# Two out-projection pieces moved into the recurrence, and VectorE's low parts moved ahead of the convolution's centring

## What is computed

```python
for l in range(DEPTH):                      # DEPTH = 2
    x = x + 0.5 * _swiglu(_rms_norm(x, norm_ffn1[l]), ...)
    proj = _rms_norm(x, norm_mix[l]) @ w_in[l]
    y_rwkv = _rwkv7_mixer(p_rwkv, ...)      # 384 columns: recurrence over time, norm over each head
    y_attn = _attention_mixer(...)          # 384 columns
    y_conv = _conv_mixer(...)               # 256 columns
    mix = concatenate([y_rwkv, y_attn, y_conv])
    x = x + mix @ w_out[l]                  # the out projection
    x = x + 0.5 * _swiglu(_rms_norm(x, norm_ffn2[l]), ...)

def _conv_mixer(u, dw_w, dw_b, ln_w, ln_b):
    z = depthwise causal convolution, 31 taps, of u[:256] * sigmoid(u[256:])
    mu = mean(z); var = mean(square(z - mu))        # over the 256 channels
    return silu((z - mu) * rsqrt(var + CONV_LN_EPS) * ln_w + ln_b)
```

## Time and profile before

| | |
|---|---|
| Median of 3 runs | 1378.06 us (1377.97 to 1378.1) |
| The profiled execution, its own time | 1380.12 us |
| Its span in the trace | 1378.3 us |
| TensorE (PE) busy | 1348.3 us, 98% of the span |
| VectorE (DVE) busy | 980.0 us, 71% |
| ScalarE (ACT) busy | 741.7 us, 54% |
| GpSimd (POOL) busy | 156.2 us, 11% |
| Mean granted TensorE clock | 0.993 |

### The profile page before, as it was taken

How to read it: one execution, slowest core, us unless ns; L and a number is a source line. 1 busy time by engine, 2 the same in 40 slices (tenths; PEclk the granted TensorE clock), 3 DMA queues, 4 the chain that set the end, 5 groups by cost and what they waited for, 6 DMA issues and landing times.

```text
span 1378.3 us, 24757 instructions
## 1 busy us (share of the span) xinstructions
PE 1348.3 (98%) x9701; PEld 1168.5 (85%) x9701; DVE 980.0 (71%) x1310; ACT 741.7 (54%) x1048; POOL 156.2 (11%) x156
## 2 busy tenths in 40 slices
PE   9999999989999999999999998999999999999997
PEld 7888889977888888888888987788888997788885
DVE  6666666777776666766656766876666665998787
ACT  6444457465744445644447656564444445755553
POOL 3000000097000000000000048300000033000000
PEclk9999999999999999999999999999999999999999
DMA  9756355123475645755529121465553953456630
GB/s 339 265 184 197 112 178 174 34 92 114 150 251 189 197 130 184 261 189 183 183 67 298 55 93 34 127 225 197 187 187 106 305 183 106 152 187 216 197 133 31
DMA packets 170483, 230.57 MB, mean 167 GB/s; under 512 B 4687, under 2 KB 151815, under 8 KB 170149
## 3 DMA queue, kind: packets, MB, share of 16 engines
q1 hardware_dynamic: 167920, 223.75, 49.6%
q10 hardware_dynamic: 1877, 5.59, 1.1%
q0 software_dynamic: 608, 0.12, 0.1%
HBM read 228.39 MB, written 2.63 MB: 168 GB/s over the span
## 4 chain that ended last, share of the span: by engine, by line
PE 89%; DVE 5%; ACT 3%; issue 1%; POOL 1%; ACTq 0%; POOLq 0%; DVEq 0%
PE banks L490 37%; PE banks L658 27%; PE banks L662 14%; PE banks L1530 2%; DVE down_lo L475 1%; DVE gate_lo L475 1%; PE banks L613 1%; PE banks L941 1%; PE banks L1180 1%; PE banks L1393 1%; PE banks L1333 1%; PE banks L1190 1%; DVE up_lo L475 1%; PE banks L1464 0%; PE banks L1202 0%
## 5 line engine op out<-in xcount | busy, mean ns | idle before, releaser
L658 PE MATMUL banks<-hT,up_hi 128*128 128x512 f32 x880 | 220.8, 393 | 0.0
L475 DVE TENSOR_TENSOR down_lo<-w_down,down_hi 128x2048 fp32r<-128x2048 f32 (+1 forms) x65 | 147.8, 2273 | 93.2 <-ACT down_hi L470 93.2
L737 ACT ACTIVATE work<-banks 128x256 f32<-128x256 f32 x176 | 66.8, 384 | 258.6 <-PE banks L662 258.2
L658 PE MATMUL banks<-hT,gate_hi 128*128 128x512 f32 x800 | 199.8, 392 | 0.0
L470 ACT ACTIVATE down_hi<-w_down 128x2048 fp32r<-128x2048 f32 (+1 forms) x65 | 123.6, 1902 | 115.9 <-PE banks L490 115.9
L658 PEld LDWEIGHTS banks<-hT,up_hi 128*128 128x128 f32 x880 | 158.2, 189 | 29.2 <-issue 0.6
L475 DVE TENSOR_TENSOR up_lo<-w_up,up_hi 128x2048 fp32r<-128x2048 f32 x72 | 164.5, 2285 | 15.9 <-ACT up_hi L470 15.9
L475 DVE TENSOR_TENSOR gate_lo<-w_gate,gate_hi 128x2048 fp32r<-128x2048 f32 x64 | 146.9, 2296 | 36.7 <-ACT gate_hi L470 36.6
L658 PEld LDWEIGHTS banks<-hT,gate_hi 128*128 128x128 f32 x800 | 147.0, 188 | 28.4
L490 PE MATMUL banks<-down_hi,ff_hi 128*128 128x512 f32 x400 | 156.2, 391 | 0.0
L490 PE MATMUL banks<-down_lo,ff_hi 128*128 128x512 f32 x400 | 156.2, 391 | 0.0
(11 more groups left out here) (388 smaller groups left out, 2217.4 us busy)
## 6 DMA issues: line engine op xcount, KB each, us to landing
w_up<-in_ffn_w_up_dram SPq DMA_DIRECT2D x44, 1024.0 KB, 5.4
w_down<-in_ffn_w_down_dram SPq DMA_DIRECT2D x44, 1024.0 KB, 5.2
w_gate<-in_ffn_w_gate_dram SPq DMA_DIRECT2D x43, 1024.0 KB, 5.4
w_up<-in_w_in_dram SPq DMA_DIRECT2D x12, 1024.0 KB, 9.5
w_gate<-in_w_up_dram SPq DMA_DIRECT2D x11, 1024.0 KB, 5.0
w_up<-in_w_up_dram SPq DMA_DIRECT2D x11, 1024.0 KB, 5.1
w_down<-in_w_down_dram SPq DMA_DIRECT2D x11, 1024.0 KB, 5.0
w_down<-in_w_in_dram SPq DMA_DIRECT2D x9, 1024.0 KB, 8.4
```

The lines of the kernel that those rows point to most:

```text
L475: dve.tensor_tensor(staged[kind][1][:, 0:cols], slot[sl][:, 0:cols], staged[kind][0][:, 0:cols].bitcast(F32), ALU.subtract).then_inc(split ...
L658: pe.matmul(bank[:, :], w[0][:, c, at], hpair[:, :, c, :], start=c == 0, stop=False)
L737: act.activation(to[:, q, j * SEQ:(j + 1) * SEQ], psum[2 * q + j][:, SEQ:], ACT.Copy)\
```

## The change

Three things move; no operation is added or removed. Of the four pieces `out_unit(1, 1, t, h)` that stood behind the convolution's mean, the two of the first token tile now stand in the recurrence's last two chunks. The two pieces `out_unit(1, 0, 0, h)`, which need the recurrence's low parts, stood behind the variance product and now stand ahead of it. On VectorE the two low parts of the recurrence's rows now precede the centring.

```diff
@@ PE, in the recurrence's loop over ch
                     y_of(0)
                     y_of(1)
                     values_of(1)
+                    out_ready(1, 2)
+                    out_unit(1, 1, 0, 0)
                 if ch == 3:
                     y_of(2).then_inc(S["y_mm"], 1)
+                    out_unit(1, 1, 0, 1)
@@ PE, behind the convolution's mean
             mm.then_inc(S["cl_mean"], 1)
-            out_ready(1, 2)
-            for t, h in HALVES:
-                out_unit(1, 1, t, h)
+            for h in range(2):
+                out_unit(1, 1, 1, h)
+            out_ready(1, 4)
+            for h in range(2):
+                out_unit(1, 0, 0, h)
             pe.wait_ge(S["cl_sq"], 1 + past["cl_sq"])
...
             mm.then_inc(S["cl_var"], 1)
-            out_ready(1, 4)
-            for h in range(2):
-                out_unit(1, 0, 0, h)
             out_ready(2, 4)
@@ DVE
+            for k in range(2):
+                dve.wait_ge(S["mix_high"], k + 3 + past["mix_high"])
+                dve.tensor_tensor(parity(hT[1][:, 0:3, :])[:, k], parity(mix[:, 0:3, :])[:, k],
+                                  parity(hT[0][:, 0:3, :])[:, k].bitcast(F32), sub).then_inc(S["mix_low"], 1)
             dve.wait_ge(S["cl_mean"], 1 + past["cl_mean"])
             for c in range(2):
                 ins = dve.scalar_tensor_tensor(mix[:, 6 + c, :], psum[0][:, 0:SEQ], -1.0 / 256, mix[:, 6 + c, :], mult, add)
             ins.then_inc(S["conv_dve"], 1)
-            for k in range(2):
-                dve.wait_ge(S["mix_high"], k + 3 + past["mix_high"])
-                dve.tensor_tensor(parity(hT[1][:, 0:3, :])[:, k], parity(mix[:, 0:3, :])[:, k],
-                                  parity(hT[0][:, 0:3, :])[:, k].bitcast(F32), sub).then_inc(S["mix_low"], 1)
             dve_low(dve, uses, OUT_SLOTS[2], kind=OUT_KINDS[2])
```

## The result

Median of five runs after the change: 1384.39 us (1384.26 to 1386.31); five runs of before on the same chip: 1378.06. The ratio is 1.0040, 95% interval 1.0022 to 1.0058. The side that was predicted holds. The size is met less well: 1384.39 is 2.4 us above the predicted 1382.0 and 0.2 us above the range of 1376.8 to 1384.2, though inside the forecast's own 1380.6 to 1384.5. Of the two terms one, the wait for the square, is right nearly to the tenth, and the other, the clock, isn't, as the experiments show.

What follows compares the result with a forecast made beforehand. TensorE, busy 98% of the span, was taken as the bound. A net loss of 1.95 us per mixer, 3.9 in both, gave 1384.0 for the profiled execution and 1382.0 for the median; range 1376.8 to 1384.2.

Steps and rivals of the forecast that it cites:

- The square behind the low part: Ahead of the variance product: GpSimd's square, blocked by VectorE's weight-tile low part, makes TensorE wait 2.2 us.
- The strict form of the rule: Square fully blocked until the low part ends: ends 346.85, slot 2 at 347.8, each mixer loses 0.2 us.
- The rival with an unblocked square: Square not blocked, no clock fall: slot 2 waits for the tile's low part, starts 1.5 us earlier; 1375.1 us, chance 0.10.
- The order then, at full clock: From the recurrence's end to slot 2, without half clock: mean near 340.2, slot 2's pieces at 347.4 instead of 347.63.
- Each mixer gains about 0.2 us: Whole mixer with full clock throughout, against the trace of before: 0.2 us gained each, 0.5 in all.
- the fall at 335.3: First mixer, behind the recurrence's small products: before's 6.8 us of half clock, expected to go; chance 0.05 that it stays.
- Behind slot 2 nothing new waits: Behind slot 2: root, ScalarE's next tile and silu come some 1 us later, yet TensorE arrives about half a microsecond after them.
- net 1.95 a mixer: At or round the new wait: a 6.8 us clock fall costs 2.15 us, less 0.2 gained; both mixers, chance 0.38.
- the clock was whole through the wait: Sign against the forecast: no half clock during TensorE's new wait ahead of the variance product, expected about 2.2 us long.

Runs made afterwards that it cites:

- the waiting low part: The changed kernel, with VectorE waiting for GpSimd's square ahead of the weight tile's low part: 1378.09 us against 1379.0 for before, ratio 0.9993.
- the repeat: The changed kernel, unaltered, timed again later against before on the same chip: 1382.31 us against 1379.0, ratio 1.0024.
- the first comparison: The first timing of the changed kernel against before, five runs each on one chip: 1384.39 us against 1378.06, ratio 1.0040.
- the tail alone: The changed kernel without the two pieces in the recurrence; all four stand behind the mean again: 1382.69 us against 1379.0 for before, ratio 1.0022.
- the filled wait: The changed kernel with nine unread products of 512 columns put into TensorE's wait for the square: 1382.7 us, ratio 1.0026 against before.

## Why the prediction was right, and where it wasn't

**The square behind the low part: right.** Predicted: it lasts 2.8 to 3.1 us, ends 0.8 to 1.0 after the low part, TensorE idles for 2.2. Measured: 3.02 and 0.90 in every profile in which the tile's low part follows the centring at once, and 2.10 in both of the change. The strict form of the rule (the Trainium skill, "SBUF — State Buffer", "Who interferes with whom") needs a whole square behind the low part, which is the 1.04 us that it takes alone; the trace has 0.14 less. The 1.28 that the prediction took for it holds a short block of its own: in before the square becomes ready 0.16 us after the first short low part has started, and ends 0.90 after that one's end (344.86 and 343.97), just as it does behind the long one. That the exclusion exists, and that it is between these two engines, the runs with ScalarE's square and with the waiting low part show from both sides. The rival with an unblocked square (1375.1) is out. Its idea of what would then come, slot 2 waiting for the tile's low part, is seen in the run with ScalarE's square (0.43) and where the low part was made to wait (1.28). The gain that the prediction put there, 1.5 us a mixer over the trace of before, is no more than 0.5 to 0.6 against before at full clock (28.9 and 28.8 us to slot 2, and 29.4).

**The order then, at full clock: right.** The mean was to begin near 340.2 and began at 340.45, slot 2 at 347.4 and began at 347.59. The stretch before had run 0.5 late, with a wait of 0.64 us for "issue" at L1557 that before doesn't have, so from the mark on slot 2 came 0.3 sooner than forecast (30.5 us, not 30.8).

**"Each mixer gains about 0.2 us": the step that failed.** It set the new order at full clock against before's order at half clock, as if the fall at 335.3 came in every execution. It doesn't. Before at full clock reaches slot 2 in 29.4 us and not in 31.0, so the change loses 1.1 to 1.2 a mixer there. That both mixers fell in the same place looked like proof, but it was one execution, and of the four profiles with TensorE's and VectorE's order of before two show both falls and two show neither. The times on record pointed there: the profiled execution of before, with a clock of 0.993, lay 2.06 above the median, and of the 106 later executions of before only 17 had a clock of 0.993 or less. A gain worked out against that trace can't be added to the median of all.

**"Behind slot 2 nothing new waits": wrong in the second mixer.** I followed the variance to slot 3 and stopped there. The chain goes on over ScalarE's queue to the next part's first norm, 1.3 us more of a wait.

**The clock, "net 1.95 a mixer": wrong.** The forecast took 4.3 us from falls, 3.9 net of the gain. The waits alone cost 3.3 to 3.4. A fall came behind the new wait in both mixers in the first profile, but 3.4 us long and just behind it, not over it, and in none in the second. In both profiles the clock was whole through the wait, which the prediction named as a sign that it is wrong. Nor is the clock lower on the whole: on the repeat's chip it was 0.9961 over eleven executions of the change and 0.9950 over 31 of before. What differs is the price of a fall. In before, 13.6 us of half clock cost 3.4 us of span (1374.9 to 1378.3), since VectorE's chain covers part. The change's two spans differ by 6.2 (1378.3 to 1384.5), of which 1.1 lies ahead of the first mark, the wait for "issue" among it; the other 5.1 go with the same 13.6 us of half clock, half of which, 6.8, would be the price with nothing to cover them. Whether the idle time makes a fall likelier stays open. For it speak five executions at a mean of 0.9938 in the first comparison, and that in two more profiles a fall began within 1.5 us of the end of a long wait (883.4 behind 2.8 us in the kernel with VectorE's order alone, 901.2 behind 1.9 us at L941 in that with the tail alone). The highest mean clocks also belong to kernels that lack the wait for the square (0.9976 where the low part waits, 0.9974 in the change's order with ScalarE's square). Against it speak the repeat, the filled wait, and the order of before with ScalarE's square, which idles as little as those and had 0.9962 and 0.9959.

So that the size came near is partly luck, as two errors cancel: the waits and the order entered the sum as a gain of 0.4 us (0.2 a mixer, rounded to 0.5 in places) and cost 3.3, and the falls were booked at a loss of 4.3, where what comes on top of the 3.3 is nothing in the repeat and 3.0 in the first comparison.

## What to carry to other kernels

Ask of each instruction that is moved not only what it waits for, but what it will stand beside: on this chip a GpSimd operation that becomes ready 0.16 us after VectorE has started on a 2.28 us tile costs 1.7 us more. The same operation on ScalarE gave back the change's whole loss, and a wait of VectorE for it 2.0 of the 3.3 us at the same granted clock. Before a dip of the clock is booked to a place, take a second profile of the same program, and compare orders at the same granted clock. Follow what comes late until it meets slack; a chain over another engine's queue can come back 14 us later (from 881.2 to 895.2 here).

## What the runs showed of the hardware

- One program, two profiles: 13.6 us at half clock or none, in both orders (spans 1378.3 and 1374.9; 1384.5 and 1378.3), and 1377.1 and 1373.0 for the order of before with ScalarE's square. The stretches measured 3.4 or 6.8 us. They began among the small products of the recurrence and its norm or in the piece next to them (334.4, 335.3, 870.3, 871.2, 877.0), within 1.5 us of the end of a wait of 1.9 to 2.8 us (347.9, 883.4, 887.2, 901.2), around 750 to 754 us in or just behind products of 256 columns, and once at 853.4.
- In some executions TensorE waits 0.6 to 1.2 us at L1557 for "issue", in the change's first profile and not in its second; rows of the waits of the kernel with the recurrence pieces alone:

```profile
PE banks L1680 <- POOL proj L2153: 2.1, 2, 1.0
PE banks L1557 <- issue: 0.9, 1, 0.9
```
  It was seen in five profiles of the eight with the pieces in the recurrence, and in none of the six others. In these five a transfer of 16 KB of instructions begins 8.0 to 8.4 us after the one before it (at 314.9 us in the change's first profile), and in the other nine 4.9 to 5.3 us after it (at 311.9 in the change's second). Why it is late, no run here shows.
- GpSimd's square of 128 x 512 takes 1.04 us alone, 1.28 beside two short VectorE operations, and 3.02 behind a long one. In both of the last it ends 0.90 us after the VectorE operation that had started 0.16 us ahead of it. The second short one in turn is held by the square (1.86 for the two, where 1.24 is their time). ScalarE's takes 0.64 beside the same long one, and that isn't lengthened (2.28).
